# Down-weight loads held until the rows gathered for the expert two steps ahead are there

## What is computed

```python
for e in range(N_EXPERTS):
    he = jax.nn.silu(h2 @ w_gate[e]) * (h2 @ w_up[e])
    moe = moe + combine[..., e:e + 1] * (he @ w_down[e]).astype(jnp.float32)
x = x + moe.astype(x.dtype)
```

## Time and profile before

| | |
|---|---|
| median of 3 runs | 452.24 us (451.46 to 453.07) |
| the profiled execution | 450.83 us, of which the span from first to last instruction is 449.0 us |
| TensorE busy | 421.5 us, 94% of the span |
| VectorE, ScalarE, GpSimd busy | 273.3, 197.7, 125.9 us |
| granted TensorE clock, mean | 0.975 |
| queue q1 (SyncE's loads) | 71.97 MB, 43.4% of 16 DMA engines' span |
| queue q0 (GpSimd's) | 18.93 MB, 12.0% |

### The profile page before, as it was taken

How to read it: one execution, slowest core, us unless ns; L and a number is a source line. 1 busy time by engine, 2 the same in 40 slices (tenths; PEclk the granted TensorE clock), 3 DMA queues, 4 the chain that set the end, 5 groups by cost and what they waited for, 6 DMA issues and landing times.

```text
span 449.0 us, 7775 instructions
## 1 busy us (share of the span) xinstructions
PE 421.5 (94%) x2927; PEld 366.0 (82%) x2927; DVE 273.3 (61%) x655; ACT 197.7 (44%) x485; POOL 125.9 (28%) x207
## 2 busy tenths in 40 slices
PE   7899999999999998999998999999999998999970
PEld 3786999997876866888895988999999997899950
DVE  3855232616778987364258796555577775497770
ACT  6475222505576664232124433344455554366340
POOL 2010000200242415251001304333335543466431
PEclk9999999999999999999998999999999999899995
DMA  7841605306000089613226599998899999963120
GB/s 268 302 160 47 223 1 182 111 1 195 1 1 2 1 334 364 261 52 149 89 93 244 178 403 392 379 361 352 354 360 355 344 369 352 349 231 120 55 81 21
DMA packets 32073, 91.36 MB, mean 203 GB/s; under 512 B 11200, under 2 KB 11712, under 8 KB 27942
## 3 DMA queue, kind: packets, MB, share of 16 engines
q1 hardware_dynamic: 20790, 71.97, 43.4%
q0 software_dynamic: 11248, 18.93, 12.0%
HBM read 86.38 MB, written 26.01 MB: 250 GB/s over the span
## 4 chain that ended last, share of the span: by engine, by line
PE 61%; issue 12%; DVE 7%; POOL 7%; DMA 6%; ACT 5%; POOLq 0%; SPq 0%; DVEq 0%; ACTq 0%
PE ps L1188 13%; PE ps L822 9%; PE ps L824 9%; PE ps L823 9%; DMA region_x<-h_rows,lists 5%; PE ps L1125 2%; PE ps L1181 2%; PE ps L1205 2%; PE ps L1206 2%; PE ps L1210 2%; PE ps L943 2%; PE ps L978 2%; POOL region_x L699 2%; DMA region_x<-in_x_prompt 1%; POOL mix L699 1%
## 5 line engine op out<-in xcount | busy, mean ns | idle before, releaser
L1188 PE MATMUL ps<-region_p,region_a 128*128 128x128 f32 x512 | 59.1, 276 | 0.6 <-DVE region_p L2025 0.6
L1188 PEld LDWEIGHTS ps<-region_p,region_a 128*128 128x128 f32 x512 | 57.9, 192 | 1.2 <-DVE region_p L2025 1.1
L824 PE MATMUL ps<-region_a_r,region_w_r 128*128 128x288 f32 x192 | 56.5, 294 | 0.0
L699 POOL DMA_INDIRECT region_x<-h_rows,lists x13 | 22.1, 1700 | 77.6 <-DVE slot_w L2123 77.6
L822 PE MATMUL ps<-region_a_r,ring_r 128*128 128x288 f32 x128 | 40.5, 317 | 0.0
L823 PE MATMUL ps<-region_a_r,ring_r 128*128 128x288 f32 x128 | 37.7, 295 | 0.0
L1575 ACT ACTIVATE region_p<-ps,gffn_sb 128x128 f32<-128x128 f32 x116 | 31.5, 382 | 10.9 <-PE ps L1181 10.9
L824 PEld LDWEIGHTS ps<-region_a_r,region_w_r 128*128 128x128 f32 x192 | 36.1, 188 | 0.0
L1596 ACT ACTIVATE region_t<-ps 128x256 f32<-128x256 f32 x16 | 6.1, 382 | 56.1 <-PE ps L1188 56.1
L1188 PE MATMUL ps<-region_p,ring 128*128 128x128 f32 x256 | 29.6, 277 | 0.6 <-DVE region_p L2047 0.4
L822 PEld LDWEIGHTS ps<-region_a_r,ring_r 128*128 128x128 f32 x128 | 24.0, 188 | 6.9 <-issue 3.3
(11 more groups left out here) (358 smaller groups left out, 1025.8 us busy)
## 6 DMA issues: line engine op xcount, KB each, us to landing
region_a<-in_w_gate SPq DMA_DIRECT2D x8, 1024.0 KB, 8.3
region_a<-in_w_up SPq DMA_DIRECT2D x8, 1024.0 KB, 13.2
region_a<-in_w_down SPq DMA_DIRECT2D x8, 1024.0 KB, 14.7
region_w<-in_w_in SPq DMA_DIRECT2D x2, 2048.0 KB, 10.2
region_w<-in_w_out SPq DMA_DIRECT2D x2, 2048.0 KB, 8.0
ring<-in_w_gate SPq DMA_DIRECT2D x4, 1024.0 KB, 9.2
ring<-in_w_up SPq DMA_DIRECT2D x4, 1024.0 KB, 13.9
ring<-in_w_down SPq DMA_DIRECT2D x4, 1024.0 KB, 13.1
```

The costliest lines, as they stand in the source:

```text
L699: pool.indirect_dma_start(out=dst, out_offset=None, in_=src, in_offset=bass.IndirectOffsetOnAxis(ap=at, axis=0), bounds_check=bound[n], oo ...
L824: return pe.matmul(out, lhs_lo, rhs_hi, start=False, stop=last)
L1188: ins = pe.matmul(ps[:, 2 + b, (first + c) * P:(first + c + 1) * P], w[:, k, c * P:(c + 1) * P], xT[:, b, k, :], start=(k == 0), stop=(k = ...
```

## The change

One wait is added to SyncE's program. At i = 1 to 11, after the wait for the down matmuls and ahead of the down load of expert i+3, SyncE also waits until the gather of the rows of expert i+2 has landed. `xg_loaded[0]` counts the gathers of the even experts and `xg_loaded[1]` those of the odd ones, 16 for each.

```diff
                 load_gate_up(i % RING, expert_at(i + RING))
                 if i >= 1:
                     sp.wait_ge(down_done, 2 * i)
+                    sp.wait_ge(xg_loaded[i % 2], 16 * ((i + 2) // 2 + 1))
                     load_down((i - 1) % RING, expert_at(i - 1 + RING))
```

## The result

The changed kernel took 447.54 us as the median of four runs (446.62 to 451.56), against 452.65 for the kernel before in the runs beside it: ratio 0.990, 95% interval 0.986 to 0.994. A repeat on another occasion gave 0.992 (0.989 to 0.996). So the change makes the kernel about 0.9% faster, some 4 us.

A forecast was written before the change was run, and what follows sets the result against it. TensorE, busy 94%, bounds the kernel, with some 4.9 us lost to late gathers on full DMA engines. 450.8 - 0.3 - 0.3 + 0 = 450.2 us profiled, 451.6 us as median: no change; range 448.2 to 454.2.

The forecast's parts named there:

- The stretch, the stall and its worth: Expert stage, chiefly step 11: TensorE idle 2.43 us for expert 12's row gather, then clock loss; late gathers cost 4.9 us.
- The lengths of three holds: SyncE's added wait before its down loads: 0 to 3.3 us at i = 8, 6.4 at 9, 7.4 at 11.
- the sign under which the prediction called itself wrong: In the changed kernel's profile: expert 12's gather under 14 us, or a wait for a weight load turning up.
- What the hold takes off the gather: SyncE's held down loads stand behind gate and up in q1, so holding them gains expert 12's gather 0, bounds 0 to 4.3 us.
- the working for i = 9: Expert 13's up load landed at 371.5, expert 11's gather at 368.1, before it; so the hold changes nothing for that gather.
- The gathers are late because the DMA engines are full: Steps 10 and 11: DMA engines busy 1.00 and 0.97 of the time, gathers taking 14.0 to 16.2 us.
- Step 11: Transposes for expert 12, waiting for their gather: gain 0 of the 4.3 us lost, the step staying near 15 us.
- Step 12: The hold at i = 10 lets q1 run dry, so expert 13's gather comes sooner: gain 0.3 us (0 to 0.3).
- Expert 3's transposes: Step 2: the hold at i = 1 outlasts expert 5's up load, removing 0.27 us idle: gain 0.3 us (0 to 0.3).
- Weights: Held weight loads still land before their copies on ScalarE: cost 0 unless holds add up, then up to 4.7 us.
- The first rival: Gathers do get their room and step 11's stall goes: 447.3 to 449.7 us, middle 448.5; chance 0.30.
- the second rival: Weights become the bound: q1 stays 7.7 us late until expert 7, stalling step 7's gate matmuls; 453.9 to 456.9 us; chance 0.12.

## Why the prediction was wrong

**What held.** The stretch, the stall and its worth: 4.9 us hung on late gathers, and 4.1 of them came back. The lengths of three holds: 3.2, 6.5 and 7.8 us at indices 8, 9 and 11 (each from the end of its step to the issue), forecast as 3.3 at most, 6.4 and 7.4. The one at 10 was 4.2 us and not 9.7, since its gather had become faster, and that is the sign under which the prediction called itself wrong (the gather of expert 12 under 14 us). The gather of expert 11 wasn't faster (14.1 against 14.0), and with the waits at 10 and 11 alone the gather of expert 12 took 15.8 us: to hold the load behind gate and up gives next to nothing to the gather that is under way. This fits the rule of ring order that the Trainium skill gives in "DMA: Bandwidth & Descriptors", section "Queues, rings and completion order"; the runs agree with it, by these numbers. The weights cost nothing: no run showed a wait for them, even with expert 11's load 7.3 us late.

**The step that failed** is the one headed "What the hold takes off the gather". It asked of each hold only what it does for the gather that it waits for, found for i = 10 that this is nothing, and put the gain at 0, where 4.3 us were measured. But the stalled gather is not helped by its own hold; it is helped by the one before. GpSimd's queue is in order too (in the kernel before, the gather of expert 12 landed at 382.4, the next store of partial sums at 389.2 and their gather at 392.7, as they were issued): between the gathers of experts 11 and 12 stand two stores of finished rows, the partial sums' store and their gather. What these gain at index 9, the gather of expert 12 inherits. I had used just this inheritance for index 10 (the gather of partial sums, then that of expert 13), and not one index earlier.

**The second error** is in the working for i = 9: the up load landed at 371.5 and the gather at 368.1, "before it", so the held load was taken to be behind gate and up all the time. But 371.5 is the landing on the last engine alone. Of the 32 counts of expert 13's gate and up loads in the kernel before, 25 had come by 368.5. The prediction wrote down that an engine which is done early leaves room, with bounds of 0 and 4.3 us, and took the lower end; the runs gave the upper, by the hold at i = 9. A load also lands some time after its issue even when nothing is ahead of it: in the kernel before, the down load of expert 15, issued at 399.30, was alone in its queue and still took 5.6 us to land, a row that I hadn't used.

```profile
region_w<-in_w_down SPq DMA_DIRECT2D x1, 1024.0 KB, 5.6
```

(That is the view of DMA issues from 399.0 to 399.5.) In the changed kernel the first count that the trace has of expert 12's down load, issued at 367.1, came at 373.7, where it came at 368.9 before; of the counts of the up load of expert 13 that this trace has, the last is at 370.1. So q1 stood partly empty in step 10, which its share shows: 59.2% instead of 76.3%. How much of that room came up on the engines where q0 was behind, no row shows by itself.

**What it left unasked.** "The gathers are late because the DMA engines are full" is half of the cause. With the rows placed over both halves the engines were as full in step 10, and the gathers came in time; so what made them late was how the bytes of GpSimd's queue were dealt, which the 16 counts of a gather had hinted at.

**The terms.** Step 11: 0 forecast, 4.3 us measured, the mis-sized term. Step 12: -0.3 forecast, +0.3 measured: TensorE now waits for the gather of expert 13, to which it comes 5.5 us sooner while the gather lands 5.0 us sooner. Expert 3's transposes: -0.3 forecast, -0.1 measured and within the scatter. Weights: 0 and 0. The first rival had the mechanism, and named the hold at i = 9 as what would speak for it; its price was 447.3 to 449.7 with 2 us coming back in step 12, and 447.54 lies in it. Only some 0.3 us came back, because the gather of partial sums, on which that return hung, had come sooner with the rest of the queue: the last count that the trace has is 15.1 us after its issue, not 20.1, and VectorE's addition for expert 10 began at 386.73:

```profile
386.73 1.28 DVE L2147 SCALAR_TENSOR_TENSOR mix<-ps,slot_w,mix 128x1024 f32<-128x1024 f32 x1 [2.39 <-DMA mix<-summed_rows,lists]
```

In the second rival's sum the clock term is off: at step 11's ratio (1.9 us of clock for 2.4 us idle) 2.9 us idle cost 2.3 us more and not 1.8, which makes 457.4 instead of 456.9. Nothing hung on it, since no run showed that wait.

**What stays open.** How often an execution of the kernel before has the stall, and how long: its undisturbed runs of one session go from 449.5 to 455.8 us, and only single ones are profiled. Why the waits at indices 10 and 11 alone, and those at all indices but 9, still gave some 2 us. And whether the wait adds anything once the rows are placed evenly.

## What to carry to other kernels

Room on shared engines goes to everything that stands in the other queue: when a load is held for a transfer, follow that queue up to the transfer that stalls, not only to the one that is waited for. A landing is that of the last engine; most of a load's counts can come well before it, and leave room where they do. And when one queue is late on full engines, look first at whether its bytes are dealt evenly: one changed pattern did here what eleven waits did.

## What the runs showed of the hardware

- The 16 counts of a row gather came in two groups, 3.0 to 5.1 and 12.2 to 16.2 us, when the used rows lay in the lower partitions. With the rows in both halves they came at 4.7 to 7.3 us, as far as the trace has them, with the same 18.93 MB in the queue over the whole execution.
- A stall's price in clock isn't steady. After 2.43, 2.32 and 2.02 us idle the granted clock of the step was 0.89, 0.89 and 0.88, part of it at the lower of its two levels (1.2 GHz), and the step took 15.3, 15.1 and 14.8 us; after 1.97 us idle it stayed at 1.00 and the step took 13.2 us.
- A load of 1 MB with nothing ahead of it in its queue took 5.6 us from issue to landing, while the other queue was at work. With others ahead of them in the queue, six such loads of the kernel before took 10.5 to 17.2 us.
- In step 10 of the kernel before, with the engines busy all the time, SyncE's queue had 76% of their time and GpSimd's 24%; with one load of 1 MB held, 59% and 30%.
